# Stick-breaking attention layer: scores issued a slot earlier, ScalarE's, VectorE's and GpSimd's work re-ordered within each slot

## What is computed

```python
h = rmsnorm(x, norm_g)
q, k, v, gate = split(h @ w_in, 4)
for each head, each block of 128 queries:
    z = q k^T / 8                      # 128 x 1024, strictly causal mask
    log_beta = log_sigmoid(z)
    log_1m = where(mask, log_beta - z, 0)
    after = reverse_cumsum(log_1m) - log_1m
    a = where(mask, exp(log_beta + after), 0)
    o = a v
y = (o * silu(gate)) @ w_out
out = rmsnorm(x + y, final_g)
```

## Time and profile before

| | us |
|---|---|
| median of 3 runs | 702.24 |
| lowest, highest | 701.27, 702.49 |
| time of the profiled execution | 702.83 |
| its span, first to last instruction | 701.0 |
| PE busy | 673.1 |
| DVE busy | 483.1 |
| ACT busy | 426.4 |
| POOL busy | 308.0 |

### The profile page before, as it was taken

How to read it: one execution, slowest core, us unless ns; L and a number is a source line. 1 busy time by engine, 2 the same in 40 slices (tenths; PEclk the granted TensorE clock), 3 DMA queues, 4 the chain that set the end, 5 groups by cost and what they waited for, 6 DMA issues and landing times.

```text
span 701.0 us, 10872 instructions
## 1 busy us (share of the span) xinstructions
PE 673.1 (96%) x3426; PEld 565.2 (81%) x3426; DVE 483.1 (69%) x636; ACT 426.4 (61%) x795; POOL 308.0 (44%) x225
## 2 busy tenths in 40 slices
PE   5999999999999999999999999999999997999995
PEld 4787888888888888888888888888888776888884
DVE  5835657786678676867677667766776798735565
ACT  5614757676767676767676767666766674622322
POOL 2122544555464546454655464546363643315100
PEclk9999999999999999999999999999999998999998
DMA  7131310141114111510042014201421148522342
GB/s 284 46 95 41 94 43 16 63 119 32 31 57 124 31 32 37 135 39 22 23 135 60 15 31 120 75 15 30 120 60 30 60 136 295 201 91 90 121 146 95
DMA packets 28122, 57.64 MB, mean 82 GB/s; under 512 B 3376, under 2 KB 3376, under 8 KB 28080
## 3 DMA queue, kind: packets, MB, share of 16 engines
q1 hardware_dynamic: 25312, 51.13, 24.2%
q10 hardware_dynamic: 2736, 6.03, 2.3%
q0 software_dynamic: 32, 0.00, 0.0%
HBM read 37.23 MB, written 11.53 MB: 70 GB/s over the span
## 4 chain that ended last, share of the span: by engine, by line
PE 67%; DVE 12%; POOL 10%; issue 7%; ACT 3%; DMA 1%; POOLq 0%; DVEq 0%; ACTq 0%
PE proj_ps L486 31%; PE t_ps L644 8%; PE o_ps L632 8%; PE z_ps L561 8%; DVE rest L1016 7%; PE z_ps L581 5%; POOL a_group L1115 5%; POOL w_split L1091 5%; PE proj_ps L561 4%; PE o_ps L486 2%; DVE aT L1000 1%; DMA a_group<-x 1%; ACT stage L719 1%; ACT gate L776 1%; DVE gate L982 1%
## 5 line engine op out<-in xcount | busy, mean ns | idle before, releaser
L486 PE MATMUL proj_ps<-hT,w_split 128*128 128x512 f32 x1464 | 359.9, 394 | 2.1 <-DVE hT L889 1.4
L486 PEld LDWEIGHTS proj_ps<-hT,w_split 128*128 128x128 f32 x1464 | 269.9, 188 | 57.6 <-DVE hT L889 2.3
L1115 POOL TENSOR_TENSOR a_group<-a_group,rest 128x128 f32<-128x128 f32 (+7 forms) x128 | 160.6, 1257 | 279.2 <-DVE rest L1016 279.2
L1016 DVE TENSOR_TENSOR_SCAN rest<-rest,restart 128x128 f32<-128x128 f32 (+7 forms) x128 | 213.4, 1668 | 16.0 <-ACT rest L809 15.5
L1091 POOL TENSOR_TENSOR w_split<-w_raw,w_split 128x512 fp32r<-128x512 f32 x64 | 115.6, 1807 | 38.0 <-DVE w_split L851 38.0
L1000 DVE TENSOR_TENSOR aT<-t_ps,aT 128x512 fp32r<-128x512 f32 (+2 forms) x160 | 93.2, 607 | 40.1 <-ACT aT L794 38.8
L794 ACT ACTIVATE aT<-t_ps 128x512 fp32r<-128x512 f32 (+2 forms) x160 | 80.2, 532 | 65.8 <-PE t_ps L644 64.6
L581 PE MATMUL z_ps<-arena 128*128 128x512 f32 (+2 forms) x384 | 96.3, 366 | 0.3 <-DVE arena L938 0.3
L938 DVE TENSOR_TENSOR arena<-stage,arena 64x512 fp32r<-64x512 f32 x64 | 43.9, 686 | 69.4 <-ACT arena L739 68.8
L644 PE MATMUL t_ps<-ident,a_group 128*128 128x128 f32 x576 | 84.9, 275 | 4.7 <-POOL a_group L1115 4.4
L809 ACT ACTIVATE rest<-z_ps 128x128 f32<-128x128 f32 (+7 forms) x128 | 83.9, 655 | 8.9 <-PE z_ps L581 8.6
(11 more groups left out here) (86 smaller groups left out, 454.2 us busy)
## 6 DMA issues: line engine op xcount, KB each, us to landing
w_raw<-w_in SPq DMA_DIRECT2D x64, 256.0 KB, 2.7
arena<-arena SPq DMA_DIRECT2D x32, 256.0 KB, 4.3
wo_raw<-w_out SPq DMA_DIRECT2D x16, 256.0 KB, 3.7
o_hi_scratch<-o_split SPq DMA_DIRECT2D x14, 256.0 KB, 2.1
o_lo_scratch<-o_split SPq DMA_DIRECT2D x14, 256.0 KB, 2.4
hT<-o_hi_scratch SPq DMA_DIRECT2D x14, 256.0 KB, 4.9
hT<-o_lo_scratch SPq DMA_DIRECT2D x14, 256.0 KB, 5.8
a_group<-x SPq DMA_DIRECT2D x14, 256.0 KB, 3.4
```

The source lines that it names most:

```text
L486: mm = nc.tensor.matmul(bank[:, :], w_split[:, ring, wl, b, :], hT[:, hl, b, half * HALF:(half + 1) * HALF], start=(b == 0 and n == 0), st ...
L1016: nc.vector.tensor_tensor_scan(span, span, restart[:, S - 1:(S - 1 - width if width < S else None):-1], 0.0, ALU.mult, ALU.max).then_inc(s ...
L1115: nc.gpsimd.tensor_tensor(a, a, rest[:, s % 2, S + 1 - width:S + 1], ALU.mult).then_inc(a_ready, 1)
```

## The change

It re-orders the work within slots and changes no operation. PE issues the scores of slot s+1 after the projection of slot s and ahead of its product with v (slot 15 issues the next pair's first block). ACT's first sigmoid comes right behind the evacuation, its second behind the high parts of the transposes, then the high parts of k or q and the gate. DVE begins each slot with the scan, then output sum, low parts of transposes, low parts of k or q, gate. POOL does `lo_w` in odd slots in place of the unit's second and third.

PE's slot:

```diff
             def slot(p, par, s):
-                q_late = is_first(p) and s == 0
-                if q_late:
-                    project_part(p, s)
-                if not is_tail(p):
-
-                    for block in {0: (s, s + 1), 1: ()}.get(s % 8, (s,)):
-                        scores(p, par, block)
                 if v_t_at(p, s) is not None:
...
-                if not is_tail(p) and s in proj_slots(p) and not q_late:
+                if not is_tail(p) and s in proj_slots(p):
                     project_part(p, s)
...
+
+                if is_first(p) and s == 0:
+                    scores(p, par, s)
+                if s < SLOTS - 1 and not is_tail(p):
+                    scores(p, par, s + 1)
+                elif not is_last(p) and not is_tail(p):
+                    scores(p + 1, 1 - par, 0)
 
                 for t, av, ahh, grp, j in av_at(p, s):
```

ACT's slot (the lines of k and q, the gate and the two sigmoids leave their old places):

```diff
                     to_stage(proj_ps, h, half)
-                    if kind in "kq":
-                        act.wait_ge(stage_ready, h + 1)
-                        heads_hi(kind, 1 - par, half)
-                if gate_at(p, s):
...
+                if not is_tail(p):
+                    i = s % 8
+                    width, first = P * (i + 1), z_offset(i)
+                    z, beta = z_ps[s % 2][:, first:first + width], a_g[i // GQ][:, i % GQ, 0:width]
+                    act.wait_ge(z_ready, SLOTS * p + s + 1)
+                    wait(act, a_ready, SLOTS * p + s - 1)
+                    nc.scalar.activation(rest[:, s % 2, S - width:S], z, ACT.Sigmoid,
+                                         scale=-SCALE).then_inc(rest_ready, 1)
                 if s % 4 == 1 and av_at(p, s - 1) and (not is_tail(p) or s < 9):
...
                     nc.scalar.activation(to, t_ps[t % 2][:, rel * P:HALF], ACT.Copy).then_inc(t_hi, 1)
+                if not is_tail(p):
+                    nc.scalar.activation(beta, z, ACT.Sigmoid,
+                                         scale=SCALE).then_inc(beta_ready, 1)
+                if evac and evac[0] in "kq":
+                    kind, half, h = evac
+                    act.wait_ge(stage_ready, h + 1)
+                    heads_hi(kind, 1 - par, half)
+                if gate_at(p, s):
...
                 if s in (2, 6) and not is_first(p):
```

DVE's slot (the lines of k and q and of the gate, and the scan, leave their old places):

```diff
             def slot(p, par, s):
...
+                if not is_tail(p):
+                    width = P * (s % 8 + 1)
...
+                    dve.wait_ge(rest_ready, SLOTS * p + s + 1)
+                    nc.vector.tensor_tensor_scan(span, span, restart[:, S - 1:(S - 1 - width if width < S else None):-1],
+                                                 0.0, ALU.mult, ALU.max).then_inc(scan_done, 1)
                 if s % 4 == 1 and av_at(p, s - 1) and (not is_tail(p) or s < 9):
...
                     nc.vector.tensor_tensor(lo, t_ps[t % 2][:, rel * P:HALF], hi.bitcast(F32), ALU.subtract
                                             ).then_inc(t_lo, 1)
+                evac = evac_at(p, s)
+                if evac:
+                    kind, half, h = evac
+                    if kind in "kq":
+                        heads_lo(kind, 1 - par, half, half, 4 * p + 5 + half + (2 if kind == "q" else 0))
+                if gate_at(p, s):
...
                 if s in (2, 6) and not is_first(p):
```

POOL's slot:

```diff
                 nc.gpsimd.tensor_tensor(a, a, rest[:, s % 2, S + 1 - width:S + 1], ALU.mult
                                         ).then_inc(a_ready, 1)
-                if s % 4 in (1, 2) and not is_last(p):
-                    n = 2 * (UNITS0 + 4 * p + s // 4 + 1) + s % 4 - 1
-                    lo_w(n, (UNITS0 + 1 + s // 4) % 2, s % 4 - 1)
+                if s % 2 and not is_last(p):
+                    part = s % 4 // 2
+                    lo_w(2 * (UNITS0 + 4 * p + s // 4 + 1) + part, (UNITS0 + 1 + s // 4) % 2, part)
```

More of the change, by code:

```diff
@@ L794, in slot @@
                     nc.scalar.activation(to, t_ps[t % 2][:, rel * P:HALF], ACT.Copy).then_inc(t_hi, 1)
+                if not is_tail(p):
[6 more added lines that the diff above has]
+                if gate_at(p, s):
+                    half, number = gate_at(p, s)
+                    act.wait_ge(stage_ready, evac[2] + 1)
+                    wait(act, o_gated, number - 1)
+                    nc.scalar.activation(gate[:, half * HALF:(half + 1) * HALF], stage[:, half, :],
+                                         ACT.Sigmoid).then_inc(gate_sig, 1)
                 if s in (2, 6) and not is_first(p):
@@ L803, in slot @@
                     return
[L805 to L812, removed]
                 if v_t_at(p, s) is not None:
@@ L971, in slot @@
             def slot(p, par, s):
-                evac = evac_at(p, s)
-                if evac:
-                    kind, half, h = evac
-                    if kind in "kq":
-                        heads_lo(kind, 1 - par, half, half, 4 * p + 5 + half + (2 if kind == "q" else 0))
-                if gate_at(p, s):
-                    half, number = gate_at(p, s)
-                    dve.wait_ge(gate_sig, number + 1)
-                    cols = slice(half * HALF, (half + 1) * HALF)
-                    nc.vector.tensor_tensor(gate[:, cols], stage[:, half, :], gate[:, cols], ALU.mult
-                                            ).then_inc(gate_ready, 1)
+                if not is_tail(p):
+                    width = P * (s % 8 + 1)
+                    span = rest[:, s % 2, S - 1:(S - 1 - width if width < S else None):-1]
+                    if is_first(p) and s == 0:
+                        dve.wait_ge(restart_ready, 1)
+                    dve.wait_ge(rest_ready, SLOTS * p + s + 1)
+                    nc.vector.tensor_tensor_scan(span, span, restart[:, S - 1:(S - 1 - width if width < S else None):-1],
+                                                 0.0, ALU.mult, ALU.max).then_inc(scan_done, 1)
                 if s % 4 == 1 and av_at(p, s - 1) and (not is_tail(p) or s < 9):
@@ L1001, in slot @@
                                             ).then_inc(t_lo, 1)
+                evac = evac_at(p, s)
[4 more added lines that the diff above has]
+                if gate_at(p, s):
+                    half, number = gate_at(p, s)
+                    dve.wait_ge(gate_sig, number + 1)
+                    cols = slice(half * HALF, (half + 1) * HALF)
+                    nc.vector.tensor_tensor(gate[:, cols], stage[:, half, :], gate[:, cols], ALU.mult
+                                            ).then_inc(gate_ready, 1)
                 if s in (2, 6) and not is_first(p):
@@ L1009, in slot @@
                     return
[L1011 to L1017, removed]
                 if v_t_at(p, s) is not None:
```

## The result

| | before | after |
|---|---|---|
| median of 6 runs each, us | 702.17 | 705.89 |
| lowest to highest | 701.27 to 702.49 | 705.84 to 706.76 |
| span of the profiled execution | 701.0 | 703.9 |

The ratio is 1.0061, with a 95% interval of 1.0050 to 1.0071: the change makes the kernel slower, by 3.7 us at the medians and 2.9 in the profiled spans. The forecast was 710.6 (8.4 slower), range 699 to 717: right in sign and in the range, more than twice too large.

What follows compares the result with a forecast made beforehand. PE bounds the kernel, busy 673.1 of 701 us, so only its idle time and slow stretches could be saved. Terms 7.0 + 0 + .5 - .4 + 1.3 = 8.4 on the 702.24 median gave 710.6, range 699 to 717.

Steps and rivals of the forecast that it cites:

- Slower, because the low part stands behind the scan in slots 7 and 15: PE would wait there for DVE's low part, about 1.5 and .5 us; this mechanism got a chance of 0.72.
- break-even: Rival: slot 7 stalls .3 instead of 1.5, half A is even, pair 7 decides: 702 us; chance 0.06.
- Half A, +1.2 each: Pairs 1 to 6: slot 7 stalls 1.5 us, transposes start at 306.5 instead of 305.32; 7.0 us in all.
- Half B, 0: Slot 15: the chain from scores to low part stalls PE .5 us, against the old .5; 0 for each of 7.
- Late weights, "Nothing": `lo_w` behind products 5 and 7 instead of 5 and 6: scan 7 gains nothing, the later load has time; cost nothing.
- the old .4: The earlier kernel's estimated PE stall in each half A, expected to vanish within the new slot 7 stall.
- k, q, gate late, nothing: These operations are due a slot or more later, covered by the next slot's projection; nothing, except pushing the port.
- Pair 7, half A, -0.4: Stalls of 1.2, 2.2, 3.0, .9 in slots 5 to 8 replace gaps of 1.25 and 4.16; net -.4, ends -3 and +2.5.
- Pair 7, half B, +1.3: Slot 13 stalls .45, slot 15 1.5, and the old .5 goes; +1.3 us, between 0 and 2.
- The waits just go: Rival: slot 7's low part lands by 300.9, so PE never waits and the kernel is faster, 691.5 us; chance 0.17.
- The clock did not fall: Answers a rival: gaps of 1.5 once a pair lower the clock, six times 2.5 us on top, 726; chance 0.05.

Runs made afterwards that it cites:

- late weights alone: Kernel before the change with only its `lo_w` moved to the odd slots; 697.66 us, ratio 0.9937.
- the kernel with the short multiply: Changed kernel, but POOL's gate multiply of slot 5 covers 64 of 512 columns, the other 448 left without the gate; 705.91 us, ratio 1.0056.
- late weights with the late gate product in pair 7: Kernel before with `lo_w` in odd slots, and in pair 7 DVE's gate product behind the low parts of the transposes; 696.55 us, ratio 0.9920.

## Why the prediction was right, and where its sizes were not

**Slower, because the low part stands behind the scan in slots 7 and 15: right.** The waits are on L998 in these slots, the product's are gone, pair 7 has several gaps; putting the low parts first in these slots takes 6.3 us away (705.89 to 699.55). The range held this result, but it was wide enough to hold break-even as well, and the three terms that missed most (half A, half B, half B of pair 7) were all forecast too high.

**Half A, +1.2 each: measured +0.75.** Counted from the first transposes, scan 7 ended 0.34 sooner than the turns said, so the stall was 1.17 and not 1.5; .26 of it hides the wait for the evacuation, since taking the stall away gains .91. With the cover that the evacuation lost (35.85 against 35.68 with late weights alone: .17) and without the old stall (36.01 against 35.68: .33, estimated at .4) that is .91 + .17 - .33 = .75. The mechanism was right, and this term was mis-sized.

**Half B, 0: measured -0.2 each.** The new stall costs .07 (in two pairs .3), because it lies where PE waits for the evacuation anyway (266.31 + .60 is when the bank is free, and the product with v starts at 266.64); the old one was 0.39 (35.39 against 35.00).

**Late weights, "Nothing": the step that failed.** The prediction said that the `lo_w` of slot 6 came after scan 7, so that scan 7 gains nothing, and counted nothing. After scan 7 it stood ahead of product 7, on which PE's wait of the earlier trace rows rests. Alone the move gives 4.2; in the changed kernel undoing it costs 7.1, since `lo_w` then also holds up scan 15. The prediction had this gain in its sum without seeing whose it was: it let "the old .4" vanish in the new stall, and took the port for free in half B. That the sum came out in the range in spite of this is luck. The chain of waits of the kernel before named the operation, with 5% of the span.

**k, q, gate late, nothing:** PE waits for them no longer after than before (0.3 us once, on a low part of k or q, in both), so nothing speaks against it; it was not tried alone.

**Pair 7, half A, -0.4: close (-0.1) by luck.** The gap of 1.25 went, as forecast (half B of pair 6 is 1.3 shorter). In slots 5 to 8 the gaps are 1.14, 1.55, 2.68 and none, against 1.2, 2.2, 3.0 and .9 forecast, and .59 in slot 1 was not forecast; the prediction also left out that slots 5 and 6 had .51 and 1.18 before. So the gaps within the half hardly change in sum (5.85 before, 5.96 after), and the half is 1.2 longer because the lower clock now falls on PE's work in it: in the kernel with the short multiply, at full clock and with gaps of 5.8 in sum, it takes 31.02.

**Pair 7, half B, +1.3: measured -0.6**, the worst of the small terms. Slot 15 has its stall (1.09, forecast 1.5) and the loads of o cost 0.50. But the old half B also held the slow stretch behind 585.86, which the prediction put at .8 + 1.7 and left standing; before, the granted clock was 0.50 until 591; after, it is 0.61 from 586 to 590 and 0.96 from 590 to 594, and most of that lies ahead of 589.35, in half A. Half B keeps .4 of it (transposes 1.50 for 1.07).

**The rivals.** "The waits just go" asked that scan 7 end 1.5 sooner; counted from the first transposes it ended 0.4 sooner (32.29, before 32.70). The clock did not fall at gaps of 1.0 in pairs 1 to 6 (the page after has PEclk 9 in all slices but the last, mean 0.994). Of the 8.2 us that the change costs on top of late weights, the low parts in slots 7 and 15 are 6.3; no run takes the other 1.9 apart.

**The port.** The Trainium skill ("SBUF — State Buffer", Who interferes with whom) says that the two engines hold the pair of ports exclusively; the disturbed scans shown here agree (2.29 alone, 3.12 and 3.28 behind the other's operation).

## What to carry to other kernels

Before costing a re-ordering, read the chain for operations that are on it and not due: here 5% of the span was a weights operation ahead of a product that PE waited for, and moving it alone gained 4.2 us (the chain's share points at the operation; what it is worth is nearer to PE's wait for the product, 4.4 us). Where two engines share a resource, lay out the turns by issue time; removing 1 us moved nothing in pairs 1 to 6 until the order of the turns changed. And parts of a re-ordering price each other: with the scan first (slots 7 and 15 aside) the kernel takes 752.9 with the old order of scores and 699.6 with the new one. The best version found is late weights with the late gate product in pair 7, 696.55, and late weights alone, 697.66, is all but as good.

## What the runs showed of the hardware that was not expected

- The port goes to the operation that was issued first, but what is issued while it is held waits inside its own duration: a scan of 128 elements, issued at 303.11 in the changed kernel behind product 7 (303.02), took 2.19, and 0.41 in the kernel with late weights alone (300.31), where it was issued just ahead of the product. Cutting a gate multiply from 1.30 to 0.33 let `lo_w` be issued 0.23 ahead of scan 6 and made the scan longer, 2.94 instead of 2.68.
- Gaps of 1.0 once a pair left the granted clock at full; behind gaps of 2.68 and 4.16 it was 0.61 and 0.50 over the next microseconds. The length of one gap does not settle it: behind a gap of 2.67 in the same place, with the gate multiply short, the clock stayed at 1.00, and with late weights and the late gate product, where the longest gap is 1.78, it fell to 0.50 (582 to 586). What decides between them stays open.
